# Experts' products as four tiles of 32 stationary columns, and the shared expert's gate-up product formed ahead of the ranks

## The reference, cut to what matters

```python
def swiglu(h, wg, wu, wd):
    return (jax.nn.silu(h @ wg) * (h @ wu)) @ wd

# moe_ffn, for h of (512, 1024)
scores = sigmoid(h @ router_w)                  # 64 experts in 8 groups
top_e = top_k(where(emask, scores + bias, -inf), 8)   # emask: the best 4 groups
gw = scores[top_e] / sum(scores[top_e]) * 2.5
y[tok] += swiglu(h[tok], exp_gate[e], exp_up[e], exp_down[e]) * gw
return y + swiglu(h, sh_gate, sh_up, sh_down)
```

## Time and profile before

| what | value |
|---|---|
| median of three runs | 2841.64 us |
| the profiled execution's own time | 2839.84 us |
| its span, first to last instruction | 2837.4 us |
| PE busy | 2664.7 us (94%), 11777 MATMULs |
| DVE, ACT, POOL busy | 1276.7 (45%), 450.3 (16%), 428.2 us (15%) |
| mean granted TensorE clock | 0.976 of full |
| HBM read and written | 462.47 and 68.73 MB |
| line 2872 and line 2874, busy PE | 1005.3 and 527.3 us |

### The profile page before, as it was taken

The page is one execution under the profiler, slowest core; times in us unless marked ns, Lnnn a source line. Parts: engine busy times, 40 slices in busy tenths (PEclk is TensorE's granted clock), DMA queues, the critical chain, the costliest instruction groups (busy, mean ns, idle before and its releaser), DMA issues. The chain is left out here.

```text
span 2837.4 us, 30729 instructions
## 1 busy us (share of the span) xinstructions
PE 2664.7 (94%) x11777; PEld 1211.9 (43%) x11778; DVE 1276.7 (45%) x2404; ACT 450.3 (16%) x889; POOL 428.2 (15%) x779
## 2 busy tenths in 40 slices
PE   6998899999999999889999959999999999999995
PEld 3445648778547883446874531111111111111112
DVE  3469636666124336873443483333223333233324
ACT  1024611211001004252320100000000000000001
POOL 0022001210000001000000023222222222222204
PEclk9999999999999999999999879999999999999998
DMA  7411005562403971021031118356555445436617
GB/s 321 200 52 60 1 31 207 210 221 82 155 24 142 404 278 60 15 91 46 3 123 58 52 56 369 141 191 234 204 213 201 157 181 196 162 122 236 279 40 289
DMA packets 71163, 433.12 MB, mean 153 GB/s; under 512 B 16228, under 2 KB 16884, under 8 KB 46994
## 3 DMA queue, kind: packets, MB, share of 16 engines
q0 software_dynamic: 39488, 245.00, 22.7%
q1 hardware_dynamic: 31570, 186.65, 17.1%
HBM read 462.47 MB, written 68.73 MB: 187 GB/s over the span
## 5 line engine op out<-in xcount | busy, mean ns | idle before, releaser
L2872 PE MATMUL psum<-arena 128*32 128x512 f32 x2016 | 1005.3, 612 | 21.2 <-DMA arena<-in_exp_gu,arena 20.3
L2874 PE MATMUL psum<-arena 128*32 x1008 | 527.3, 605 | 0.0
L965 PE MATMUL psum<-arena 128*128 128x256 f32 x1904 | 417.0, 381 | 2.6 <-PEq L1005 1.7
L965 PEld LDWEIGHTS psum<-arena 128*128 128x128 f32 x1904 | 361.6, 191 | 63.3 <-issue 14.6
L2872 PEld LDWEIGHTS psum<-arena 128*32 128x32 f32 x2016 | 165.7, 121 | 452.2 <-issue 451.1
L2947 DVE STREAM_TRANSPOSE arena<-arena 32x256 f32<-32x256 f32 x688 | 299.5, 435 | 18.3 <-DMA arena<-scratch_h,arena 9.4
L2874 PEld LDWEIGHTS psum<-arena 128*32 128x32 f32 x1008 | 69.2, 108 | 409.8 <-issue 409.8
L2958 DVE TENSOR_TENSOR arena<-arena,psum 128x256 f32<-128x256 f32 x42 | 17.7, 422 | 412.2 <-ACT arena L2921 412.2
L2953 DVE COPY arena<-psum 128x512 f32<-128x512 f32 x42 | 29.1, 692 | 300.0 <-PE psum L2874 300.0
L1067 PE MATMUL psum<-arena 128*128 128x512 f32 x352 | 151.8, 592 | 0.3 <-PEq L1091 0.3
L2921 ACT ACTIVATE arena<-psum 128x256 f32<-128x256 f32 x42 | 16.1, 384 | 724.3 <-PE psum L2874 724.3
(11 more groups left out here) (572 smaller groups left out, 2948.8 us busy)
## 6 DMA issues: line engine op xcount, KB each, us to landing
scratch_expert_out<-arena SPq DMA_DIRECT2D x18, 2048.0 KB, 20.5
arena<-in_w_ada SPq DMA_DIRECT2D x12, 2048.0 KB, 17.3
arena<-in_ada_w POOLq DMA_DIRECT2D x12, 2048.0 KB, 8.6
arena<-in_w_up SPq DMA_DIRECT2D x22, 1024.0 KB, 4.9
scratch_expert_out<-arena SPq DMA_DIRECT2D x42, 512.0 KB, 2.7
arena<-in_w_in SPq DMA_DIRECT2D x9, 2048.0 KB, 10.3
arena<-in_w_down SPq DMA_DIRECT2D x5, 2048.0 KB, 8.5
arena<-in_w_o SPq DMA_DIRECT2D x2, 2048.0 KB, 8.3
```

Source lines behind the costliest of these rows:

```text
L965: last = pe.matmul(out, w[:, k, :], x[:, k, :], start=(k == 0), stop=(k == KH - 1))
L2872: pe.matmul(bank[r, :], left[:, r], weights[:, OWN, col:col + 512], start=first, stop=last_)
L2874: return pe.matmul(bank[0:GUEST, :], left[:, 0:GUEST], picked, start=first, stop=last_)
```

## The change

`rows_of` now splits the 128 rows into four tiles of 32 stationary columns instead of 32, 64 and 32: the tile of 64 becomes two calls of 32. In `phase_route`, the two `shared_product` calls on DVE move from behind line 2744 to just behind their definition, ahead of line 2718.

```diff
@@ phase_route, vector
                 sh_mul.by(tt(act_h[:, m, :], hg[:, m, :], K.bank[6 + m], ALU.mult))
 
+            shared_product(0)
+            shared_product(1)
+
             spread_e = lambda x: x[:, :].unsqueeze(1).to_broadcast([P, NT, EXPERTS])
             step(ts(limit[:, :], own[:, :], float(BLOCK), None, ALU.mult))
...
             for t in range(NT):
                 step(dve.max(slot_f[:, t, :], tmp[:, t, :]))
-            shared_product(0)
-            shared_product(1)
             sf = slot_f[:, :, :].rearrange("p t j -> p (t j)")
...
@@ phase_experts, tensor, rows_of
-                for r in (slice(GUEST, 2 * GUEST), slice(2 * GUEST, P)):
+                for r in (slice(m, m + GUEST) for m in range(GUEST, P, GUEST)):
                     pe.matmul(bank[r, :], left[:, r], weights[:, OWN, col:col + 512], start=first, stop=last_)
```

## The result

The changed kernel takes **2322.28 us** (median of 4 runs, 2320.63 to 2324.6) against 2841.9 us for the kernel before on the same chip (4 runs, 2840.84 to 2846.02): a ratio of 0.817, interval 0.8156 to 0.8184. The forecast was 2334, and the range of 2290 to 2430 holds the time. The profiled execution took 2321.17 us, with a span of 2319.2 where it was 2837.4: 518 us less.

The account below looks back on a forecast made before the run. PE was taken to bound the experts' stage, with transfers hidden. From 2839.84 us, 514 less for the stage, plus 5 for the clock and 1.4 for the moved products, gave 2332, put at 2334 against the median; range 2290 to 2430.

Parts of the forecast that it names:

- The likeliest case: Experts' stage: four tiles run at once, with DMA deciding at blocks of two experts; 2334 us, chance 71%.
- The split: Experts' products on PE: a call takes two rounds, 0.87 us; a block 10.9 us instead of 25.3, bounds 10.4 and 16.4.
- That rival (2486): Calls of `rows_of`: the register's tile lags into a third round, a block takes 16.4 us on PE; 2486 us, chance 9%.
- the one in which tiles don't overlap (3570): Calls of `rows_of`: eight passes one after another, 3.5 us a call, 42.7 a block; 3570 us, chance 2%.
- The transfers: Experts' stage from 1761 us: DMA late at blocks of two experts, 17.4 us against 10.9 otherwise; 482 us in all.
- the last block and the extra stores: Experts' stage: 10 us added to the 482, so that the stage ends at 2253 us instead of 2767.
- The rival with worse transfers (350 GB/s, 2398): Experts' stage: requests queue behind each other and DMA reaches only 350 GB/s; 546 us, 2398 in all, chance 7%.
- The clock: PE in the experts' stage: slow patches after waits at some dozen blocks cost 5 us, bounds 0 and 20.
- The moved products: DVE in the routing: standing for the second `gate_up` makes the block list net 1.4 us later; bounds 7 gained, 4 lost.
- as many collide as before: Routing: assumed that POOL's four adds, moved 7 us forward, slow as many DVE operations; 7 us gained if none collides.
- The rival with a loop fetched again each turn (2364): Experts' loop: the longer code is fetched again at each of 11 returns, 30 to 100 us; 2364, at worst 2434; chance 10%.
- low end, 2300: Whole kernel, likeliest case: 476 us instead of 482, no clock cost, 7 gained in the routing, some 10 for overlapping filling.

## Why the prediction was right

The likeliest case came, by its mechanism. The sum forecast 508 us less (2839.84 - 2332); the span fell by 518. The difference of 10 us is put together like this; in part it is as small by luck, as said below.

**The split.** Forecast 0.87 us for a call and 10.9 for a block; measured 0.86 and 32.43 / 3 = 10.8. The register's tile starts 0.02 us behind the fixed ones, in some calls up to 0.32, and never needs a third round. That rival (2486) is out, and the one in which tiles don't overlap (3570) with it.

The share taken from the Trainium skill, TensorE: Matmul & The Clock Gate, part 3, 2.38 for three column tiles, would have made a call an estimated 1.1 us; the trace has 0.86, which is eight passes of 0.43 us in two rounds, four at a time with nothing lost. The measurement decides: line 244's rounds were the better guide.

**The transfers.** Forecast for the stage from about 1760 us: 482 and 10 us; measured 489.5. The two kinds of turn were forecast as 17.4 us for a block of two experts and 10.9 otherwise. The turn from 2153.96 us shows it: 43.59 us at 427 GB/s are 18.6 MB; less 3 x 0.95 MB for tokens and outputs and divided by 3.15 MB, five experts. Two blocks of two and one of one were forecast as 2 x 17.4 + 9.9 = 44.7 us. PE waits for weights 62 us (82.2 - 20.1) in 16 waits, forecast 50 to 70 in a dozen. The runs without fetches give the same sum from the other side: 65 us come back under the new tiles, none under the old. The turn from 2089.11 us shows the running ahead that the forecast allowed for: the DMA engines are full in it, and yet PE never waits.

That the stage's end came so close is in part luck: two errors of the sum cancel. The rows count the passes of the register's tile, of which a block has 24, up to 1760 us and, in the kernel before, up to 1761 and from 2715 us on (us, busy us of PE and of weight loads with counts, clock, DMA share, GB/s; after, then twice before):

```profile
1704.50:1760.00 55.50, 35.22 (x68) 8.08 (x69) 0.81 0.99 412
1704.50:1761.10 56.60, 25.66 (x49) 3.47 (x50) 0.95 0.99 408
2715.30:2770.00 54.70, 25.82 (x50) 3.30 (x48) 1.00 0.06 26
```

The forecast took 10 us for "the last block and the extra stores" behind its last stretch, but 50 passes, two blocks, were left there: by 10.8 us a block some 22. It also let nothing move before 1761 us; there the changed kernel had 68 passes behind it instead of 49, 0.8 of a block, worth some 9 us.

The rival with worse transfers (350 GB/s, 2398) did not come: 424 and 427 GB/s in full turns, above the 416 of the earlier trace rows.

**The clock.** It fell, as forecast: 0.92 in the two turns with waits that stand above, 1.00 in the two without. A row behind a wait shows the lower level, 1.07 us for a pass instead of 0.6, in the timeline of PE; below it the stretch of the passes that follow, at a clock of 0.50 (columns as in the earlier trace rows):

```profile
2187.92 1.07 PE L2873 MATMUL psum<-arena 128*32 128x512 f32 x3 [4.86 <-DMA arena<-in_exp_gu,arena]
...
2187.92:2190.45 2.53, 2.53 (x12) 0.98 (x16) 2.46 (x6) 0.00 (x0) 1.89 (x6) 0.50 1.00 416
```

PE's busy time is 477.8 us where 42 blocks of 10.81 make 454, so 24 us more, above the upper bound of 20. But these passes stand in turns that the DMA engines set, so I read the clock as paid inside the waits; the 5 us on top of the transfers did not show in the stage's 489.5. By that reading the term was too high; no run has the waits without the lower clock.

**The moved products.** Forecast 1.4 us later; measured 0.4 sooner. The timeline of the routing after, DVE:

```profile
1643.82 0.29 DVE L2710 TENSOR_SCALAR arena<-arena 128x128 f32<-128x128 f32 x1
1644.14 0.69 DVE L2715 TENSOR_TENSOR arena<-arena,psum 128x512 f32<-128x512 f32 x1
1646.18 0.69 DVE L2715 TENSOR_TENSOR arena<-arena,psum 128x512 f32<-128x512 f32 x1 [1.35 <-PE psum L2522]
...
1651.56 2.27 DVE L2738 SCALAR_TENSOR_TENSOR arena<-arena 128x64 f32<-128x64 f32 x1
...
1655.02 2.46 DVE L2742 TENSOR_TENSOR arena<-arena 128x256 f32<-128x256 f32 x1
...
1658.66 1.01 DVE L2747 MAX8 arena<-arena 128x8 f32<-128x64 f32 x4
...
1662.02 2.16 DVE L2760 TENSOR_TENSOR arena<-arena 128x127 f32<-128x127 f32 x1
...
1684.49 0.26 DVE L2798 TENSOR_SCALAR arena<-psum 128x96 uint32<-128x96 f32 x1 [2.22 <-PE psum L2557]
```

The stand came as forecast: DVE waits 1.35 us for the second `gate_up` and is 2.6 us later at the ranks (forecast 2.7). From L2710 to the list it takes 1684.49 - 1643.82 = 40.67 us; before, it is 1685.34 - 1644.29 = 41.05 (and the row of the list in the kernel before; ahead of it two rows of its line 2790, beside POOL's adds):

```profile
1665.00 6.09 DVE L2790 TENSOR_SCALAR arena<-arena 128x96 f32<-128x96 f32 x8
...
1672.46 3.91 DVE L2790 TENSOR_SCALAR arena<-arena 128x96 f32<-128x96 f32 x8
...
1685.34 0.26 DVE L2797 TENSOR_SCALAR arena<-psum 128x96 uint32<-128x96 f32 x1 [2.22 <-PE psum L2557]
```

The step that was off is "as many collide as before". Before, each of POOL's four adds slowed something on DVE: one the cast of the earlier trace rows, the others the two rows of line 2790 (2.01 us without an add). Now three do, and the third falls mostly on the four MAX8, 1.01 us as ever. The term had the wrong sign, by 1.8 us, inside its bounds of 7 and 4.

**What is left of the 10 us.** The 5 of the clock; 2.4 because the stage begins at 1704.5 instead of 1706.9 (1705.5 + 1.4): 1.8 from the moved products, the rest because the phases ahead ended some 0.5 us sooner; 2.5 in the stage (489.5 against 492, with the two errors above in it); under 1 behind it.

**The code.** The rival with a loop fetched again each turn (2364) did not come. One reading of the earlier trace rows was off: of the six fetches of instructions in the kernel before two lie in the loop's first turn, between 1870 and 1920 us; only the later turns have none. The DMA queues of the kernel after, from 1870 to 2242 us (packets, MB, share), show no instruction queue:

```profile
q0 software_dynamic: 21027, 125.92, 84.3%
q1 hardware_dynamic: 4320, 15.73, 10.4%
```

A turn now has 298 MATMULs and 294 weight loads where it had 224 and 222, and the run without fetches has PE busy without a gap through twelve of them (648 DVE operations at 54 a turn).

**Details missed.** POOL's wait was to be "nearly gone" and is 137 us: POOL's requests still wait for PE to free a buffer, also in turns that the transfers set (24.9 us from 1821 to 1906 us). The DMA share is 0.94 rather than 0.9. The forecast's own low end, 2300, is 2305 by the terms that it names.

## What to carry to other kernels

Before trusting that an engine's gain is kept, work out for each stretch what the next engine needs: here PE's 25.3 us hid transfers of 10 or 17 us, and the maximum of the two, stretch by stretch, gave the end of the stage within 10 us, helped by two errors that cancelled. Count the blocks that are left outside the stretches, too. When tiles of unequal width share the array, count how many groups of columns work at a time; cutting all to the narrowest width can cost more instructions and still be much shorter. Once the bound has moved to transfers, the order in which they are asked for is worth looking at again: the same edit of the order gave 30 us after the change and nothing before it.

## What the runs showed of the hardware

**Four tiles of 32 columns overlap fully**, even where one of them has its operand picked by a register: four passes every 0.43 us. In the kernel before, a tile of 64 beside two of 32 did not, and ran alone for half of each call. The width of 64 alone is not what hindered it: an early product of the same kernel (line 702) has two tiles of 64 columns side by side, and its 24 passes of 128 columns of moving data take 1.53 us, in PE's timeline:

```profile
256.79 1.53 PE L702 MATMUL psum<-arena 128*64 128x128 f32 x24
```

At 0.43 us for 512 columns a pass of 128 takes an estimated 0.11 us, so 24 one after another would need some 2.6 us and twelve pairs 1.3. So it is tiles of different widths that did not run together here. Why, no row shows, and no run tried two tiles of 64 in `rows_of`.

**POOL's adds of 1024 elements slow some operations of DVE and not others.** The four adds last 2.3 to 2.6 us each. Operations of DVE that were slowed start while an add runs, mostly 0.1 to 0.8 us after its start, and end within 0.3 us of its end: TENSOR_TENSOR on 127 elements took 2.16 us here and 2.39 in the run with the product later, where it was 0.29 in the kernel before, whose row shows it without an add beside it:

```profile
1656.68 0.29 DVE L2759 TENSOR_TENSOR arena<-arena 128x127 f32<-128x127 f32 x1
```

POOL's own timeline has the adds of the kernel after:

```profile
1651.40 2.36 POOL L2591 TENSOR_TENSOR arena<-arena 128x1024 f32<-128x1024 f32 x1 [36.26 <-ACT arena L2581]
...
1658.26 2.58 POOL L2591 TENSOR_TENSOR arena<-arena 128x1024 f32<-128x1024 f32 x1 [1.07 <-ACT arena L2581]
```

The first stands over L2738 (2.27 us), the other over the MAX8, which are not slowed.

The Trainium skill, GPSIMD Engine Reference, section Specifications, says that POOL shares its SBUF interfaces with DVE, with contention where DVE's instruction has two SBUF inputs or runs in a 2-port mode. The rows agree for the three slowed here that have two inputs (L2738, L2742, L2760) and for MAX8, which has one. Others that were slowed have one input, too: the cast of the earlier trace rows, line 2790 above, and the TENSOR_SCALAR of the run with the product later. In which mode those ran, no row shows.
